# The low weight part of every fourth down-projection unit is made by an accumulating DMA

## The reference

```python
act = jax.nn.gelu(jnp.einsum('tkd,td->tk', ue, ht), approximate=False)
ve = jnp.take(v, it, axis=0)
return jnp.einsum('tk,tkd->td', gt * act, ve)
```

## Time and profile before

| | |
|---|---|
| median of 3 runs | 1412.5 us (1412.31 to 1413.71) |
| the profiled execution's own time | 1412.38 us |
| its span, first to last instruction | 1410.3 us |
| TensorE busy | 1388.3 us, 98% |
| VectorE busy | 1036.4 us, 73% |
| ScalarE busy | 735.3 us, 52% |
| GpSimd busy | 298.3 us, 21% |
| granted TensorE clock, mean | 0.998 of full |
| DMA | 279 MB, 198 GB/s over the span |

### The profile page before, as it was taken

The page is one execution under the profiler, slowest core; times in us unless marked ns, Lnnn a source line. Parts: engine busy times, 40 slices in busy tenths (PEclk is TensorE's granted clock), DMA queues, the critical chain, the costliest instruction groups (busy, mean ns, idle before and its releaser), DMA issues.

```text
span 1410.3 us, 25136 instructions
## 1 busy us (share of the span) xinstructions
PE 1388.3 (98%) x10156; PEld 1255.5 (89%) x10157; DVE 1036.4 (73%) x1841; ACT 735.3 (52%) x1070; POOL 298.3 (21%) x176
## 2 busy tenths in 40 slices
PE   9999999999999999999999999999999999999997
PEld 7989989999999999997777788888899798899985
DVE  5665574694987999998888777688777755777754
ACT  5674655545464444444444445544567654655543
POOL 5000000488862222210000031144213000000000
PEclk9999999999999999999999999999999999999999
DMA  6433356455679777765555588788443553555552
GB/s 242 150 127 127 130 170 225 149 195 195 194 250 342 242 250 251 253 219 168 178 168 170 190 294 286 262 300 316 151 150 119 165 165 105 179 180 185 189 192 92
DMA packets 76579, 279.16 MB, mean 198 GB/s; under 512 B 8496, under 2 KB 8752, under 8 KB 76208
## 3 DMA queue, kind: packets, MB, share of 16 engines
q1 hardware_dynamic: 67104, 243.73, 51.3%
q0 software_dynamic: 9216, 33.56, 6.3%
q10 hardware_dynamic: 144, 0.26, 0.0%
HBM read 276.47 MB, written 1.05 MB: 197 GB/s over the span
## 4 chain that ended last, share of the span: by engine, by line
PE 75%; issue 15%; ACT 4%; DVE 4%; POOL 1%; DMA 0%; SPq 0%; POOLq 0%; DVEq 0%; ACTq 0%
PE bank L466 74%; ACT A L1193 2%; ACT whi L1193 2%; DVE wlo L1761 1%; POOL wlo L2653 1%; PE bank L475 1%; ACT L1193 1%; DVE A L1761 1%; DVE A L1757 0%; DMA raw<-in_w_in_t 0%; DVE xres L1761 0%; ACT hTh L1193 0%; DVE small L2453 0%; DVE small L1761 0%; POOL small L2659 0%
## 5 line engine op out<-in xcount | busy, mean ns | idle before, releaser
L1193 ACT ACTIVATE whi<-raw 128x1024 fp32r<-128x1024 f32 (+1 forms) x450 | 473.3, 1054 | 390.0 <-PE bank L466 388.1
L1761 DVE TENSOR_TENSOR wlo<-raw,whi 128x1024 fp32r<-128x1024 f32 (+1 forms) x385 | 472.0, 1227 | 258.5 <-ACT whi L1193 255.9
L466 PE MATMUL bank<-hTh,whi 128*128 128x224 f32 (+1 forms) x1944 | 547.7, 282 | 2.6 <-DVE wlo L1761 1.7
L466 PE MATMUL bank<-hTh,wlo 128*128 128x224 f32 (+1 forms) x1944 | 540.1, 278 | 0.0
L466 PE MATMUL bank<-hTl,whi 128*128 128x224 f32 (+1 forms) x1944 | 540.0, 278 | 0.0
L466 PEld LDWEIGHTS bank<-hTh,whi 128*128 128x128 f32 x1944 | 370.0, 190 | 6.7 <-DVE wlo L1761 2.5
L466 PEld LDWEIGHTS bank<-hTl,whi 128*128 128x128 f32 x1944 | 370.0, 190 | 0.3 <-issue 0.2
L466 PEld LDWEIGHTS bank<-hTh,wlo 128*128 128x128 f32 x1944 | 369.9, 190 | 0.0
L466 PE MATMUL bank<-whi,hTh 128*128 128x512 f32 (+2 forms) x552 | 217.4, 394 | 0.2 <-DVE wlo L1761 0.2
L466 PE MATMUL bank<-whi,hTl 128*128 128x512 f32 (+2 forms) x552 | 214.2, 388 | 0.0
L466 PE MATMUL bank<-wlo,hTh 128*128 128x512 f32 (+2 forms) x552 | 214.2, 388 | 0.0
(11 more groups left out here) (192 smaller groups left out, 1550.4 us busy)
## 6 DMA issues: line engine op xcount, KB each, us to landing
raw<-in_u SPq DMA_DIRECT2D x128, 512.0 KB, 3.3
raw<-in_v SPq DMA_DIRECT2D x128, 512.0 KB, 3.3
raw<-in_w_up SPq DMA_DIRECT2D x44, 512.0 KB, 3.3
raw<-in_w_down SPq DMA_DIRECT2D x22, 512.0 KB, 3.3
raw<-in_w_in_t SPq DMA_DIRECT2D x17, 512.0 KB, 4.1
raw<-in_w_in_g SPq DMA_DIRECT2D x16, 512.0 KB, 3.2
raw<-in_w_out SPq DMA_DIRECT2D x16, 512.0 KB, 3.9
raw<-in_w_pq SPq DMA_DIRECT2D x16, 512.0 KB, 4.4
```

The source lines that it names most:

```text
L466: return e.matmul(o, l, r, start=st, stop=sp_, skip_group_check=True)
L1193: return e.activation(o, i, func, **kw)
L1761: return e.tensor_tensor(o, a, b, op)
```

## The change

Of the units of "v" from the twentieth on and below the 124th, those whose index in the whole stream is a multiple of four (n = 22, 26, ..., 122: 26 units) get their low part in another way. ScalarE first writes the negative of the rounded value into the low buffer (`scale=-1.0`), then the high part as before. GpSimd waits for the first of these and issues a DMA from its queue that adds the raw weights, in SBUF, to what the low buffer holds. VectorE has no `lo` for these units. TensorE waits for the DMA's semaphore, one of three in turn. The load four units later waits for the DMA, and for the high part too.

```diff
+def by_dma(i):
+
+    return 20 <= i - BASE["v"] < 124 and i % 4 == 0
+
+
 def low_table():
-    out, n = [], {"lo_dve": 0, "lo_pool": 0}
+    out, n = [], {"lo_dve": 0, "lo_pool": 0, "lo_dma": 0}
     for i in range(NU):
-        by = "lo_pool" if on_pool(i) else "lo_dve"
+        by = "lo_dma" if by_dma(i) else "lo_pool" if on_pool(i) else "lo_dve"
         n[by] += 1
+        if by == "lo_dma":
+            k = n[by] - 1
+            out.append((f"lo_dma{k % 3}", 16 * (k // 3 + 1)))
+            continue
         out.append((by, n[by]))
     return out
...
+DMA_COUNT = np.cumsum([by_dma(i) for i in range(NU)]).tolist()
...
                 if i >= NSPL:
                     e.wait_ge(s["w"], i - NSPL + 1)
+                if by_dma(i):
+                    act(W(i)[1], raw[i % NRAW][:, :], ACT.Copy, scale=-1.0).then_inc(s["neg"], 1)
                 act(W(i)[0], raw[i % NRAW][:, :], ACT.Copy).then_inc(s["hi"], 1)
...
+                elif i < NU and by_dma(i):
+                    e.wait_ge(s["neg"], DMA_COUNT[i])
+                    e.dma_start(W(i)[1], raw[i % NRAW][:, :], accum_op=ALU.add).then_inc(s[LOW[i][0]], 16)
...
                     by, n = LOW[i - NRAW]
                     e.wait_ge(s[by], n)
+                    if by_dma(i - NRAW):
+                        e.wait_ge(s["hi"], i - NRAW + 1)
```

More of the change, by code:

```diff
@@ L164 @@
 SEMS = """
-hi lo_dve lo_pool w acc0 acc1 acc2 ev_act ev_dve
+hi lo_dve lo_pool lo_dma0 lo_dma1 lo_dma2 neg w acc0 acc1 acc2 ev_act ev_dve
 n_sq n_sum n_rstd n_scaled n_scaled0 n_tr n_hi n_lo r_add r_part final half
```

## The result

The changed kernel takes 1481.3 us, the median of four runs (1478.33 to 1482.2), where the kernel before took 1412.4 beside it: 1.048 times, interval 1.046 to 1.050, or 69 us slower. The forecast was 1497, in a range from 1424 to 1600. The profiled execution took 1482.2 us, with a span of 1480.0 against 1410.3, 69.7 us more.

The account below looks back on a forecast made before the run. TensorE, busy 98% of the span, was taken to bound the kernel. Stalls of 46.9 us (17 units) and 19.6 (nine), plus 17.8 for late issues, made 84.3 on 1412.4: about 1497 us, range 1424 to 1600.

Parts of the forecast that it names:

- slack: Time from the DMA's issue until TensorE needs the low part: 4.24 us, or 4.82 in units with a gate batch.
- 26 waits: Sign expected in the profile after: TensorE waits for the DMA of the low part at 26 places.
- D: Time from issue to landing of GpSimd's adding DMA, taken as 7.0 us for every changed unit.
- What bounds, and what the relief is worth: TensorE bounds the stage; removing 26 VectorE subtractions (31.8 us) gains 0, and 26 more ScalarE activations (27.6 us) cost 0.
- T: ScalarE's start in a unit's preparing turn; the DMA was to issue at T + 1.10, TensorE to need it at T + 5.34.
- The term 17 x 2.76 = 46.9: TensorE's stalls in us in the 17 changed units without a gate batch, each 7.0 - 4.24.
- The bounds of 5.7 and 7.6: Range in us expected for the DMA's landing, with a second pass of 1.4 us for the addition's second operand.
- The nine units with a gate batch: Early changed units, turns up to 52: TensorE stalls 7.0 - 4.82 in each, 19.6 us in all.
- The rival of a quick landing: The DMA lands in 3.3 to 4.9 us, like SP's load, giving 1425 to 1442 us; chance 0.2.
- The late units: From turn 97 gathers waiting for VectorE's picks hold GpSimd: two units 4.84 us late, four 2.04, 17.8 in all.
- The load behind: SP's load four units later waits for the DMA and lands 3.5 us after issue; hidden, with 2.4 us left.
- The clock: Rival: TensorE's clock halves in stalls, 17 us for six units (1514) or 73 for 26 (1570); chance 0.1 over 30 us.

Follow-up runs that it names:

- no_low: Changed kernel with ScalarE's negative, GpSimd's DMA and the subtraction removed for the 26 units: 1413.7 us, ratio 1.0006 to the kernel before.
- neg_extra: Kernel before plus 26 ScalarE activations writing the negative, and the load's wait for the high part; VectorE still subtracts: 1412.5 us against 1413.5, ratio 0.9999.
- plain_copy: Changed kernel with GpSimd's late gathers held behind the DMA, whose addition is replaced by a copy of the raw weights: 1434.3 us, ratio 1.016.
- gate_units: Changed kernel with only the nine changed units up to n = 54: 1413.7 us against 1412.3 for the kernel before, ratio 1.0008.
- dma_first: Changed kernel, but from turn 96 on GpSimd issues the gathers of two turns behind the DMA: 1457.2 us, ratio 1.032 to the kernel before.
- no_gathers: Changed kernel without the 32 gathers of v: 1435.7 us, ratio 1.016 to the kernel before.

## Why the prediction was right, point by point

The mechanism holds: a relief that is worth nothing, and a DMA that lands later than the slack allows, later still where gathers stand in front of it. The sizes hold less well, and by the prediction's own signs it was wrong in part: it named 26 waits and there are 17, it took D near 7.0 for all and it was 4.7 in nine units (whose slack it had too short besides), it booked no wait for loads and there is one, and it wanted the clock to stay up and it fell. That the time came within 16 us of the forecast is in part luck, since errors of opposite sign met (the sum, below).

**What bounds, and what the relief is worth.** As forecast: no_low shows 0, and neg_extra shows 0 for ScalarE, both within 0.2%.

**The start of the DMA.** Taken as T + 1.10, it is T + 1.36 in the 20 units that aren't late. GpSimd needs 0.29 us from ScalarE's end to its DMA's start, not VectorE's 0.03. The slack was thus 3.98 us without a gate batch. This costs 17 x 0.26 = 4.4 us.

**The landing D, the mis-sized term.** Taken as 7.0. In the 17 units it measured 6.05 in the mean (102.9 us over the 17 pieces of the chain), and in the nine 4.7 (4.5 to 5.2). The term 17 x 2.76 = 46.9 came out as 102.9 - 17 x 3.98 = 35.2. The bounds of 5.7 and 7.6 held for the crowded part in the mean, and not for the other: one value was taken for two stretches, though the difference of DMA share, 0.51 and 0.84, stood in the earlier trace rows. The second operand was put at 1.4 us; plain_copy gives 1.2, of which 0.3 is a longer issue. What was too high was the base, 5.6: the direct copy lands after 3.4 beside the loads alone and 4.4 in the crowded part, with an issue of 0.53 to 0.56 us, where the gathers had one of up to 1.85 and landed after 6.2.

**The nine units with a gate batch.** 19.6 us forecast, 0 waited; gate_units gives 1.4 us with an interval that holds 0. Two errors made the term. One is D, 4.7 in the median and not 7.0. The other is the slack: a batch stands after every second unit, but in the changed turns two of them lie between ScalarE's start and the unit. TensorE's timeline of the kernel before shows it for T = 699.69, in whose turn unit 26 is prepared (two units, 24 matmuls, stand between two batches):

```profile
699.44 0.66 PE L466 MATMUL bank<-og,oh 128*128 128x64 f16 x16
705.62 0.66 PE L466 MATMUL bank<-og,oh 128*128 128x64 f16 x16
706.11 0.48 PE L466 MATMUL bank<-whi,hTh 128*128 128x512 f32 x1
```

The first batch has just begun at T, the second is done ahead of unit 26, and the unit starts at T + 6.42. So the DMA has 5.06 us from T + 1.36 (5.32 from the T + 1.10 of the forecast) and not 4.82. Only one landing of the nine is longer, unit 34's 5.20, and that unit starts 0.2 us late. With the slack as forecast, less the 0.26, seven of the nine landings would have come too late. The rival of a quick landing (3.3 to 4.9) about came true for these nine.

**The late units.** All six are the ones named, for the reason named. Against T + 1.36 units 102 and 114 are issued 4.57 us late (4.84 forecast) and 106, 110, 118 and 122 by 0.79 to 0.88 (2.04 forecast); 12.5 us against 17.8. The four are less late because the gather in front of them takes 0.94 to 0.96 us to issue and not the 1.85 of the kernel before. In these four VectorE does nothing during the issue, since its next subtraction waits for ScalarE and that for the stalled TensorE; at unit 102, with a subtraction beside it, the issue takes 1.76 us. Which of the two an issue takes was not tested by itself. dma_first confirms the lateness with 14.8 us of waits less.

**The load behind.** Said to be hidden with 2.4 us left, at a landing of 3.5. In two places it took 7.7 and 7.0 us, and ScalarE waited 8.3 us for loads in all. The idle time of an ordinary unit is D - 3.98 less 0.12 (unit 66: 6.62 - 4.10 = 2.52, and 2.53 stand in the trace), as the last matmul ahead of it still runs for a while. So with its D of 4.79 unit 62 would have idled 0.69 us and idled 2.45; unit 98 idled 2.10 for 1.12. This cost some 2.7 us, a wait that I booked at nothing. That gathers are its cause is shown by no_gathers, where ScalarE has no such wait.

**The clock.** It was a rival and came true in part, beside the forecast: 12.8 us by the slow matmuls, near the 17 worked out for six units. The nearness is chance: five of the six late units are among the seven groups, of them only unit 102 is slow for all its twelve matmuls, and two groups stand elsewhere. It fell ahead of 940 us as well, behind waits of 4.64 us (unit 74) and 3.41 (unit 90).

**The sum.** 84.3 forecast. Measured, D and the late issues give 35.2 + 12.5 = 47.7; with 2.7 for the late loads and 17 x 0.12 = 2.0 less for where the idle time begins, that is 48.4, and the trace has waits of 48.5. Then come the two terms that the sum didn't have, 4.8 for the broken overlap and 12.8 for the clock, and the 3.6 outside the account. So the two terms of the landing were 11.7 and 19.6 us too high and the late issues 5.3, 36.6 in all, and 22.0 us (0.8 + 4.8 + 12.8 + 3.6) were booked at nothing. The difference is the 14.6 us between 84.3 and 69.7. The total came near by luck in this sense; the waits alone, 48.5 us, are little more than half of what was forecast.

**The estimate by the Trainium skill.** By the fit in the Trainium skill ("DMA: Bandwidth & Descriptors", "Anatomy of one DMA — SWDGE (gpsimd) path") a transfer of this size takes 3.2 us, as an estimate; the plain copy here landed after 3.4 in the median beside the loads alone. With the second read that an add needs by the Trainium skill ("Collectives: The Full Stack", "The bandwidth ceiling") the estimate is 4.4, and 4.6 to 4.7 was measured beside the loads alone. Estimate and runs agree there to within 0.3 us, so it was the better base for the nine early units; the 6.05 of the crowded part isn't in the fit.

No experiment beats the kernel before, and none could by this way: TensorE had no wait in the stage that a quicker low part would end. gate_units is the form of the change that costs nothing measurable.

## What to carry to other kernels

Before work is moved off an engine, ask who waits for that engine; here nobody did, and 29 us of freed VectorE bought nothing. A DMA that stands in for an engine's instruction is to be held against the buffers' slack (here 1.2 us of work with 3 us to spare became 4.5 to 8.7 us of latency), in the stretch where it runs and with the traffic that is there. Where it is issued from an in-order queue, walk through what stands in front of it; a wait there costs its length, and if TensorE idles through it, it can cost the clock on top, as here behind seven of 17 waits.

## What the runs showed of the hardware

A direct accumulating DMA of 512 KB within SBUF, from GpSimd's queue, lands 4.6 us after its issue in the median with only the loads of weights beside it; the same as a copy takes 3.4 us, and with 256 KB added 3.8 us. Its issue keeps GpSimd 0.85 to 0.98 us in the median, that of the copy 0.53. Beside gathers of the same size the full one takes 6.0 to 6.1 us in the median. Once TensorE had idled for 6.64 us the clock was near 1.2 GHz for the whole next unit, and a unit took 5.5 us for 2.8; dummy matmuls in such gaps kept the clock and gained 8.5 us.
